# A one-core encoder layer: head loads spread over three blocks, gate stores over four tiles, a third bank for transposes

## What is computed

```python
mod = jax.nn.silu(c) @ w_ada + b_ada
sh1, sc1, g1, sh2, sc2, g2 = jnp.split(mod[:, None, :], N_MOD, axis=-1)
h = rmsnorm(x) * (1 + sc1) + sh1
z = h @ w_in
...
scores = jnp.einsum('bqhd,bkhd->bhqk', qb, k, preferred_element_type=jnp.float32)
p = jax.nn.softmax(scores, axis=-1).astype(v.dtype)
return jnp.einsum('bhqk,bkhd->bqhd', p, v)
...
x = x + g1 * (jnp.concatenate([att, pool], axis=-1) @ w_out)
h = rmsnorm(x) * (1 + sc2) + sh2
return x + g2 * expert_choice_ffn(h, w_router, w_gate, w_up, w_down)
```

## Time and profile before

| | us |
|---|---|
| median of three runs | 3889.8 |
| the three runs | 3885.39, 3889.8, 3892.07 |
| the profiled execution | 3886.55 |
| its span | 3884.8 |

### The profile page before, as it was taken

The page is one execution under the profiler, slowest core; times in us unless marked ns, Lnnn a source line. Parts: engine busy times, 40 slices in busy tenths (PEclk is TensorE's granted clock), DMA queues, the critical chain, the costliest instruction groups (busy, mean ns, idle before and its releaser), DMA issues. The chain is left out here.

```text
span 3884.8 us, 54537 instructions
## 1 busy us (share of the span) xinstructions
PE 3566.5 (92%) x19090; PEld 3095.3 (80%) x19090; DVE 2028.4 (52%) x3177; ACT 1882.6 (48%) x3261; POOL 1272.9 (33%) x1006
## 2 busy tenths in 40 slices
PE   8999798998999999979983899999999999999993
PEld 6999676666777777757762899999999999999992
DVE  3332345777888888832227544444444444444443
ACT  4333223886888888843330343443443443433433
POOL 1111045886888888942221000000000000000000
PEclk9999898998999999989995899999999999999996
DMA  7444699531222222035641445545544445445447
GB/s 244 157 157 90 208 379 330 109 69 26 50 50 44 45 44 50 6 112 179 181 149 44 152 141 162 156 146 162 151 150 138 144 151 161 152 150 162 148 122 276
DMA packets 368694, 539.12 MB, mean 139 GB/s; under 512 B 39618, under 2 KB 257010, under 8 KB 365566
## 3 DMA queue, kind: packets, MB, share of 16 engines
q1 hardware_dynamic: 340356, 448.80, 37.5%
q0 software_dynamic: 13824, 50.34, 5.4%
q10 hardware_dynamic: 14336, 37.77, 2.5%
HBM read 394.27 MB, written 142.48 MB: 138 GB/s over the span
## 5 line engine op out<-in xcount | busy, mean ns | idle before, releaser
L1531 POOL TENSOR_TENSOR att_pr<-att_e,att_pr 128x512 fp32r<-128x512 f32 x640 | 816.5, 1300 | 170.5 <-ACT att_pr L1384 161.4
L2246 POOL DMA_INDIRECT s_x<-moe_ye,moe_to_add x48 | 92.9, 1935 | 1438.1 <-DVE moe_ye L2467 1429.0
L1449 DVE TENSOR_REDUCE att_mx<-att_m_ps 128x1 f32<-128x512 f32 x640 | 423.2, 682 | 77.0 <-PE att_m_ps L1262 68.7
L2405 DVE TENSOR_TENSOR keep_wl<-keep_raw,keep_wh 128x1024 fp32r<-128x1024 f32 x380 | 440.0, 1221 | 33.6 <-ACT keep_wh L2335 33.5
L2335 ACT ACTIVATE keep_wh<-keep_raw 128x1024 fp32r<-128x1024 f32 x380 | 369.9, 1045 | 123.0 <-PE moe_d_ps L2312 123.0
L1378 ACT ACTIVATE att_e<-att_s_ps 128x512 f32<-128x512 f32 x640 | 379.0, 592 | 75.3 <-PE att_s_ps L1289 42.1
L1384 ACT ACTIVATE att_pr<-att_e 128x512 fp32r<-128x512 f32 x640 | 402.9, 630 | 17.9 <-issue 2.6
L1471 DVE TENSOR_TENSOR att_acc_ps<-att_acc_ps,att_e 128x512 f32<-128x512 f32 x544 | 374.7, 689 | 12.9 <-ACT att_e L1378 6.7
L2362 ACT ACTIVATE moe_silu<-moe_a_ps 128x384 f32<-128x384 f32 x128 | 63.0, 492 | 652.4 <-PE moe_u_ps L2285 652.4
L2443 DVE TENSOR_TENSOR moe_hf<-moe_u_ps,moe_silu 128x384 f32<-128x384 f32 x128 | 71.4, 558 | 543.6 <-ACT moe_silu L2362 543.5
L2283 PE MATMUL moe_a_ps<-moe_xh,keep_wh 128*128 128x384 f32 x1024 | 345.5, 337 | 2.1 <-DVE moe_xl L2413 2.1
(11 more groups left out here) (284 smaller groups left out, 7722.9 us busy)
## 6 DMA issues: line engine op xcount, KB each, us to landing
keep_raw<-w_gate SPq DMA_DIRECT2D x64, 1024.0 KB, 5.1
keep_raw<-w_up SPq DMA_DIRECT2D x64, 1024.0 KB, 7.6
keep_raw<-w_down SPq DMA_DIRECT2D x64, 1024.0 KB, 6.3
inp_raw<-w_ada SPq DMA_DIRECT2D x48, 512.0 KB, 6.0
s_ct<-inp_ct SPq DMA_DIRECT2D x24, 640.0 KB, 3.1
prj_ct<-s_ct SPq DMA_DIRECT2D x6, 2560.0 KB, 12.4
s_kn<-prj_out SPq DMA_DIRECT2D x24, 512.0 KB, 9.4
s_qn<-prj_out SPq DMA_DIRECT2D x24, 512.0 KB, 9.3
```

Of the source, the lines that this page charges most:

```text
L1449: nc.vector.tensor_reduce(mx[:, u % CB, u // CB:u // CB + 1], m_ps[u % MB][:, :], AX, ALU.max).then_inc(max_part, 1)
L1531: nc.gpsimd.tensor_tensor(pr[:, s % RING, 1, :], e[:, s % RING, :], pr[:, s % RING, 0, :].bitcast(F32), ALU.subtract).then_inc(lo_done, 1)
L2405: nc.vector.tensor_tensor(wl[:, s, part, :], raw[:, s, part, :], wh[:, s, part, :].bitcast(F32), ALU.subtract).then_inc(w_lo_done, 1)
```

## The change

There are three edits. The output of the program is the same.

```diff
--- before.py
+++ after.py
@@ -321,14 +321,13 @@
                 act.wait_ge(z_squared, 2 * (n + 1))
                 nc.scalar.activation(zms[:, n, :], zms[:, n, :], ACT.Sqrt, bias=eps[:, 0:1]).then_inc(z_std, 1)
 
-            def store_gates():
+            def store_gate(i):
+
+                part, g = (2, 5)[i // 2], i % 2
                 act.wait_ge(mod_done, len(EARLY) + len(LATE))
-                for a, part in enumerate((2, 5)):
-                    for g in range(2):
-                        at = (2 * a + g) * D
-                        act.dma_start(w["s_gates"][0, at:at + D].rearrange("(k p) -> p k", p=P),
-                                      keep["modc"][:, g, part * KD:(part + 1) * KD],
-                                      allow_slow_non_contiguous=True).then_inc(gates_stored, 16)
+                act.dma_start(w["s_gates"][0, i * D:(i + 1) * D].rearrange("(k p) -> p k", p=P),
+                              keep["modc"][:, g, part * KD:(part + 1) * KD],
+                              allow_slow_non_contiguous=True).then_inc(gates_stored, 16)
 
             def latent_high(n):
                 act.wait_ge(ct_ready, n + 1)
@@ -364,8 +363,8 @@
                     if b + 1 < NB:
                         modulate(b + 1, 2 * j + 1)
                     latent_high(TB * b + j)
-                    if TB * b + j == len(LATE) + 1:
-                        store_gates()
+                    if 0 < TB * b + j - len(LATE) <= 4:
+                        store_gate(TB * b + j - len(LATE) - 1)
 
         @block.vector
         def _(dve):
@@ -1150,8 +1149,8 @@
 
         @block.sync
         def _(sp):
-            def load_qk(n, i):
-                for dst, src in ((q[i][0:NOPE], w["s_qn"]), (q[i][NOPE:QK], w["s_qr"]), (k[i][0:NOPE], w["s_kn"])):
+            def load_qk(n, i, which):
+                for dst, src in ((q[i][0:NOPE], w["s_qn"]), (q[i][NOPE:QK], w["s_qr"]), (k[i][0:NOPE], w["s_kn"]))[which]:
                     sp.dma_start(dst.bitcast(F32), src[:, bass.ds(n, 1), :, tokens]
                                  .rearrange("l o r t -> (o r) l t")).then_inc(qk_in[i], 16)
 
@@ -1213,11 +1212,16 @@
             def body(it, last):
                 for b in range(NG):
                     h, j = b // NQB, b % NQB
-                    if j == 0 and from_start(it, h - 1) and not (last and h >= 1):
-
-                        sp.wait_ge(values_done, it * PER + h * NQB * NT)
-                        load_qk(it * HU + h - 1 + HU, (h - 1) % HU)
-                        load_v(it * HU + h - 1 + HU, (h - 1) % HU)
+                    if from_start(it, h - 1) and not (last and h >= 1):
+
+                        n, i = it * HU + h - 1 + HU, (h - 1) % HU
+                        if j == 0:
+                            sp.wait_ge(values_done, it * PER + h * NQB * NT)
+                            load_qk(n, i, slice(0, 2))
+                        if j == 1:
+                            load_qk(n, i, slice(2, 3))
+                        if j == NQB // 2:
+                            load_v(n, i)
                     if g and last and b == NG - 1:
                         sp.wait_ge(wp_turned, 1)
                         load_wo(PLAIN + 1)
@@ -1573,7 +1577,7 @@
         eps = m.sb("eps", [P, 1])
         h2 = m.sb("h2", [P, KD, 2 * P])
         o_ps = m.ps("o_ps", [P, 2, 2, BANK])
-        x_ps = m.ps("x_ps", [P, 2, BANK])
+        x_ps = m.ps("x_ps", [P, 3, BANK])
         l_ps = m.ps("l_ps")
         eps_set = m.sem("eps_set")
         tabs_in = m.sem("tabs_in")
@@ -1668,11 +1672,11 @@
 
                 pe.wait_ge(xn_done, 2 * r + 2)
                 for c in range(KD // 2):
-                    if c >= 2:
-                        pe.wait_ge(h2_done, KD * r + 2 * (c - 1))
+                    if c >= 3:
+                        pe.wait_ge(h2_done, KD * r + 2 * (c - 2))
                     for k in (2 * c, 2 * c + 1):
                         for u in range(2):
-                            mm = nc.tensor.transpose(x_ps[:, c % 2, (k % 2 * 2 + u) * P:(k % 2 * 2 + u + 1) * P],
+                            mm = nc.tensor.transpose(x_ps[:, c % 3, (k % 2 * 2 + u) * P:(k % 2 * 2 + u + 1) * P],
                                                      xn[:, u, k * P:(k + 1) * P], keep["ident"][:, :])
                     mm.then_inc(xn_turned, 1)
 
@@ -1729,7 +1733,7 @@
                     act.wait_ge(xn_turned, KD // 2 * r + k // 2 + 1)
                     if k == 0 and (not isinstance(r, int) or r >= 1):
                         act.wait_ge(logits_ready, r)
-                    nc.scalar.activation(h2[:, k, :], x_ps[:, k // 2 % 2, k % 2 * 2 * P:(k % 2 + 1) * 2 * P],
+                    nc.scalar.activation(h2[:, k, :], x_ps[:, k // 2 % 3, k % 2 * 2 * P:(k % 2 + 1) * 2 * P],
                                          ACT.Identity, bias=keep["modc"][:, g, 3 * KD + k:3 * KD + k + 1],
                                          scale=keep["modc"][:, g, 4 * KD + k:4 * KD + k + 1]).then_inc(h2_done, 1)
 
```

## The result

| | median us | spread of its runs | ratio to the kernel before (95% interval) |
|---|---|---|---|
| before (runs beside it) | 3889.49 | 3885.39 to 3892.07 | |
| changed kernel | 3834.69 | 3831.96 to 3837.06 | 0.986 (0.9843 to 0.9877) |

The account below looks back on a forecast made before the run. TensorE's order of work sets the time, so only its stalls, or those of engines it waits for, pay. 9.1 + 30.8 + 8.0 + 10.0 = 57.9 us off the median 3889.8 gives 3831.9; forecast 3831, range 3826 to 3841.

Parts of the forecast that it names:

- Second attention: Spreading a head's loads over blocks lets the denominators' fold go out behind an empty queue: 30.8 us off.
- B: Second attention: the stall is divided, as v alone could hold SP's next store; half of 30.8 stays, 3847 us; 8%.
- D: Both attentions: the loads are not what holds the fold, so the attentions stay as they are; 3871 us; 2%.
- Rival E: Both attentions: each block with a load pays 5.1 us, as the one does today; slower, 3941 us; 3%.
- Third bank: Output projection: a third bank for PE's transposes saves 0.91 us at each of 11 places, 10.0 us.
- Rival C: Output projection: the third bank gives nothing, the loop being held by the mix's loads or ACT; 3842 us; 5%.
- Gates: Input projection: one gate store per tile instead of four in a row; ACT doesn't wait for x, 9.1 us off.
- about 5.0 for one (an estimate, by a quarter): Input projection: four gate stores cost the x load 19.8 us, so one costs about 5.0.
- rival A: Input projection: the x load stays late, one gate store holding the DMA engines about as long as four; 3841 us; 8%.
- The turn-taking between queues: Input projection: DMA engines alternate queues by packet; read alone, x takes at worst twice its time, sum 9.1 us smaller.
- First attention: k and v loads go together at j = 1; between half and all of 9.1 us go, 8.0 taken.
- 2.1 MB need 9.5 us at 221 GB/s: First attention: k, v and a 1.05 MB part land just about in time for the fold in a 12.54 us block.

Follow-up runs that it names:

- fold_on_act: The kernel before with its loads left in place; only the fold of the denominators is issued on ACT's queue instead of SP's: 3872.09 us, ratio 0.9961.
- loads_behind: The kernel before with a head's four loads still in a row in their block, but issued behind store, fold and inverses: 3882.57 us, ratio 0.9973.
- loads_only: The kernel before with only the heads' loads spread over the blocks: 3854.98 us, ratio 0.9917.
- light_first: The changed kernel with the parts loaded ahead in the first attention reordered, row parts first, also in block 0: 3827.29 us, ratio 0.9842.

## Why the prediction was right, and where it was off

**Second attention, right** (30.6 for 30.8). The mechanism is confirmed by fold_on_act and loads_behind, and its price by loads_only. The argument had two hidden simplifications. It gave the whole wait to SP's queue, where about half was the DMA engines. And it read the price beside the 30.3 us of waits without naming the clock: 12.2 us of those waits had nothing to do with the loads and stayed, and 12.0 us of the price were the low clock after each pause of PE. That 30.3 lies so near to 30.8 is chance. Neither did harm: the price was taken from the lengths of blocks, which hold all of it, and spreading takes the whole pause away. The k load took 9.1 us at the median, not 5.9 (v 7.0); the room of 10 us covered it. Rivals B and D are out: no store of this stage is held any more, and the loads were what held the fold. Rival E's mechanism acted at two of the eight places of the first attention, and nowhere here.

**Third bank, right** (10.1 for 10.0), with the one short wait it named. Rival C is out.

**Gates, mis-sized by 1.3 us** (7.8 for 9.1). The step that failed is "about 5.0 for one (an estimate, by a quarter)". One store cost the load 18.8 − 5.7 = 13.1 us, two thirds of what four cost. So rival A pointed the right way: one store costs far more than a quarter of four, though not as much as all four. But its price was wrong too: of the 6.1 us that ACT waited for x, PE lost 1.4, and the low clock of the kernel before didn't come. The turn-taking between queues of the Trainium skill ("DMA: Bandwidth & Descriptors", section "Queues, rings and completion order"), read as equal turns, would let the load through in at worst twice its time, 11.4 us (an estimate); it took 18.8, so that reading fails here, and with the order turned round it took 5.8.

**First attention, mis-sized by 5.7 us** (2.3 for 8.0, below its bound of 4.6). Two steps failed. "2.1 MB need 9.5 us at 221 GB/s" took a rate from the middle of a transfer: from the first issue at 701.83 to v's landing at 716.5 it was 14.6 us, 143 GB/s, and the fold was issued 7.4 us after that first issue. And the sum began at 695.10, behind the block in which the stage's first loads hold the fold: over the prediction's own stretch 3.8 us went (109.46 to 105.70), and the block before it got 1.5 us longer. light_first shows what there was to be had: all of it, by another order of parts.

**The sum.** The total is 3.7 us above the forecast, inside its own range of 3826 to 3841. That it came so near is partly luck: the four terms found make 50.8 us, and the medians' 54.8 holds 4 us more that no term accounts for. The two traces alone differ by 49.5 us, 8.4 less than the 57.9 predicted; that is 7.1 of the terms, the two mis-sized ones, and 1.3 that lie outside them.

## What to carry to other kernels

A short transfer that an engine waits for can be held by what is issued before it on its queue, and by what fills the DMA engines: count the bytes in front of it, and time them from first issue to last landing, not by the rate in mid-transfer. Moving a load behind the urgent transfer only helps if whatever stands next in the queue can wait; spread loads, and put the lightest ones beside them. Price a stall by the length of the block that holds it, not by the wait that the profile names: here the low clock after PE's pauses cost 12.0 us beside 18.2 us of waits. Stores in tiny pieces belong where no load is issued for the next ten or twenty microseconds; cutting them into smaller portions helps less than their place.

## What the hardware showed

A store of 4 KB in 1,024 pieces of 4 bytes holds the DMA engines for some 8 us (20 to 33 GB/s after it), and a 1 MB load that another engine's queue got 2.9 us later took 18.8 us instead of 5.7. Four such stores hold them for 12 us or more, and cost the load 19.8 us where one cost 13.1. After a pause of PE of 2.9 us (1014 to 1017) the granted clock was 0.50 for some 3.4 us. And a DMA issue can hold its engine: behind 3.7 MB of loads a 128 KB store took SP 10.6 to 12.3 us to issue.
